# A two-model float32 stack on one core: gate products in split operands, spread rows by one stacked product, attention heads in alternation

## The reference, cut to what matters

```python
q = apply_rope(q, cos, sin) * (Dh ** -0.5)
k = apply_rope(k, cos, sin)
s_own = einsum('bhqd,bhsd->bhqs', q_c, k_own); p = softmax(where(causal, s_own, -inf))
out = einsum('bhqs,bhsd->bhqd', p, v_own)
```

```python
ig  = ml_i + ml_b_i;   lf  = log_sigmoid(ml_f + ml_b_f)      # 4 + 4 columns
flf = log_sigmoid(fx_f + fx_b_f)                             # 8 columns
cT = cumsum(flf);  s = (q @ k.T) * scale + cT[q] - cT[k]     # forgetting attention, causal
dmat = cumsum(lf)[t] - cumsum(lf)[s] + ig[s]                 # mLSTM, causal
```

## Time and profile before

| what | value |
|---|---|
| median of 3 runs | 1218.9 us |
| the profiled execution | 1219.48 us |
| its span, first to last instruction | 1217.7 us |
| TensorE busy | 1180.7 us |
| VectorE busy | 752.7 us |
| ScalarE busy | 617.7 us |
| TensorE's granted clock, mean | 0.993 |

### The profile page before, as it was taken

One profiled execution on the slowest core, in us unless ns is written; L12 is line 12 of the kernel. 1 busy time (PEld: TensorE's weight loads), 2 busy tenths in 40 slices (PEclk: granted clock), 3 DMA queues, 4 the chain that ended last, 5 costly groups with the idle time before them and its releaser, 6 DMA issues.

```text
span 1217.7 us, 24847 instructions
## 1 busy us (share of the span) xinstructions
PE 1180.7 (97%) x10598; PEld 1064.5 (87%) x10598; DVE 752.7 (62%) x1084; ACT 617.7 (51%) x892; POOL 109.5 (9%) x87
## 2 busy tenths in 40 slices
PE   6999999999999999999999999999999999999997
PEld 6797777789999989997999999799988898999996
DVE  7788775374554467785555444758478564655554
ACT  8974543363434355554643434565545474644443
POOL 0032253601100000220010000000000000000000
PEclk9999989999999999999999999999999999999999
DMA  8522111055544545333455446354432352545551
GB/s 297 209 104 72 27 53 52 20 196 217 193 186 180 206 168 183 129 119 124 173 197 186 178 169 255 109 186 173 152 126 105 138 191 104 206 177 206 188 185 42
DMA packets 29950, 188.17 MB, mean 155 GB/s; under 512 B 3489, under 2 KB 5665, under 8 KB 8737
## 3 DMA queue, kind: packets, MB, share of 16 engines
q1 hardware_dynamic: 27072, 177.21, 39.9%
q10 hardware_dynamic: 2784, 9.60, 2.4%
HBM read 185.75 MB, written 1.05 MB: 153 GB/s over the span
## 4 chain that ended last, share of the span: by engine, by line
PE 86%; DVE 8%; ACT 4%; issue 2%; DMA 0%; ACTq 0%; DVEq 0%; SPq 0%
PE ps L2046 24%; PE ps L2048 24%; PE ps L2047 23%; DVE w_lo L1333 1%; PE ps L2364 1%; PE ps L2179 1%; PE ps L2509 1%; PE ps L2369 1%; PE ps L2542 1%; PE ps L2366 1%; ACT mixed L618 1%; ACT w_hi L720 1%; PE ps L2312 1%; PE ps L2263 1%; PE ps L2762 1%
## 5 line engine op out<-in xcount | busy, mean ns | idle before, releaser
L1333 DVE TENSOR_TENSOR w_lo<-w_raw,w_hi 128x2048 fp32r<-128x2048 f32 x157 | 365.7, 2345 | 147.4 <-ACT w_hi L589 146.8
L2046 PE MATMUL ps<-x_hi,w_hi 128*128 128x256 f32 x1344 | 380.3, 283 | 4.1 <-DVE x_lo L1620 2.4
L2047 PE MATMUL ps<-x_lo,w_hi 128*128 128x256 f32 x1344 | 375.3, 279 | 0.0
L2048 PE MATMUL ps<-x_hi,w_lo 128*128 128x256 f32 x1344 | 375.1, 279 | 0.0
L589 ACT CAST w_hi<-w_raw 128x2048 fp32r<-128x2048 f32 x155 | 295.1, 1906 | 155.0 <-PE ps L2048 154.0
L2046 PEld LDWEIGHTS ps<-x_hi,w_hi 128*128 128x128 f32 x1344 | 252.6, 188 | 13.3 <-issue 8.3
L2047 PEld LDWEIGHTS ps<-x_lo,w_hi 128*128 128x128 f32 x1344 | 252.6, 188 | 2.2 <-issue 0.7
L2048 PEld LDWEIGHTS ps<-x_hi,w_lo 128*128 128x128 f32 x1344 | 252.6, 188 | 0.0
L2046 PE MATMUL ps<-w_hi,hid_hi 128*128 128x512 f32 x304 | 119.7, 394 | 0.1
L2048 PE MATMUL ps<-w_hi,hid_lo 128*128 128x512 f32 x304 | 119.4, 393 | 0.0
L2047 PE MATMUL ps<-w_lo,hid_hi 128*128 128x512 f32 x304 | 118.5, 390 | 0.0
(11 more groups left out here) (394 smaller groups left out, 1797.5 us busy)
## 6 DMA issues: line engine op xcount, KB each, us to landing
w_raw<-in_weights SPq DMA_DIRECT2D x163, 1024.0 KB, 4.9
xt<-in_xT SPq DMA_DIRECT2D x2, 512.0 KB, 5.4
w_raw<-in_weights SPq DMA_DIRECT2D x2, 512.0 KB, 6.2
x_tm<-in_x SPq DMA_DIRECT2D x1, 1024.0 KB, 5.2
gain<-in_mix_g ACTq DMA_DIRECT2D x2, 512.0 KB, 4.0
gain<-in_mix_b ACTq DMA_DIRECT2D x2, 512.0 KB, 6.0
gain<-in_ffn_g ACTq DMA_DIRECT2D x2, 512.0 KB, 7.7
gain<-in_ffn_b ACTq DMA_DIRECT2D x2, 512.0 KB, 10.8
```

What stands on the lines that cost most here:

```text
L1333: V.tensor_tensor(w_lo[:, i % WS, :], w_raw[:, i % RAW, :], w_hi[:, i % WS, :].bitcast(F32), ALU.subtract).then_inc(lo_done, 1)
L2046: nc.tensor.matmul(out, hi_l, hi_r, start=start, stop=False)
L2047: nc.tensor.matmul(out, hi_l, lo_r, start=False, stop=False)
L2048: return nc.tensor.matmul(out, lo_l, hi_r, start=False, stop=stop)
```

## The change

The input `gatesel` and its load are gone (so the count of late loads falls from 80 to 64 everywhere). The gate weights are split into `gate_hi` and `gate_lo`, each 36 columns wide (forget gates in 0 to 11, input gates in 32 to 35), which lie in parts of `mix_lo` that are free then; ScalarE and VectorE do it before ffn1. The selector `gsel` is now built on the chip in fp32r, [44, 12, 128]: VectorE adds two pieces of the identity, ScalarE copies it along 128 columns. The two gate products become one split product. The rows are split too: their high part goes to rows 0 to 11 and their low part to rows 32 to 43 of `gst_s` (`gi_s` likewise), and one fp32r product of 44 partitions with the selector, which has a one in row h and in row 32 + h, adds both. In the attentions the heads are in their natural order, slot h for head h, and the products of heads 2m and 2m + 1, which lie on different halves of the partitions, alternate.

```diff
+RS = 44
...
+        gsel = sb("gsel", [RS, 12, P], F32R, a_m)
+        sel = sb("sel", [RS, 12], where=a_m)
...
+        gate_hi, gate_lo = (mix_lo[:, n:n + 2, :].rearrange("p a b -> p (a b)")[:, 0:36 * KT].rearrange("p (k n) -> p k n", k=KT)
+                            for n in (4, 6))
+        gi_s, gst_s = mix_hi[0:RS, 6, :], mix_hi[0:RS, 7, :]
...
-            nc.scalar.dma_start(gsel[:, :], d["const_gates"]).then_inc(late_loaded, 16)
```

ScalarE, between `norm(2)` and `ffn("ffn1")`:

```diff
             load_gain("mix", 1, 2)
+            act.wait_ge(late_loaded, 64)
+            act.wait_ge(slab_done, first["moba_o"] + 4)
+            nc.scalar.copy(gate_hi[:, :, 0:12], gate_w[:, :, 0:12])
+            nc.scalar.copy(gate_hi[:, :, 32:36], gate_w[:, :, 12:16]).then_inc(gate_w_hi, 1)
+            act.wait_ge(sel_set, 1)
+            nc.scalar.copy(gsel[:, :, :], along(sel[:, :], P)).then_inc(gsel_set, 1)
             ffn("ffn1")
```

ScalarE, after the four results of ml_qk are taken:

```diff
+            act.wait_ge(gate_rows, 1)
+            nc.scalar.copy(gst_s[0:12], gst[0:12, :])
+            nc.scalar.copy(gi_s[0:4], gi[0:4, :]).then_inc(row_hi, 1)
             act.wait_ge(mem_loaded, 16)
```

VectorE, before `ffn("ffn1")`:

```diff
+            V.tensor_tensor(sel[:, :], ident[0:RS, 0:12], ident[0:RS, 32:RS], ALU.add).then_inc(sel_set, 1)
+            dve.wait_ge(gate_w_hi, 1)
+            V.tensor_tensor(gate_lo[:, :, 0:12], gate_w[:, :, 0:12], gate_hi[:, :, 0:12].bitcast(F32), ALU.subtract)
+            V.tensor_tensor(gate_lo[:, :, 32:36], gate_w[:, :, 12:16], gate_hi[:, :, 32:36].bitcast(F32), ALU.subtract)\
+             .then_inc(gate_w_lo, 1)
             ffn("ffn1")
```

VectorE, before the convolution:

```diff
+            dve.wait_ge(row_hi, 1)
+            V.tensor_tensor(gst_s[32:RS], gst[0:12, :], gst_s[0:12].bitcast(F32), ALU.subtract)
+            V.tensor_tensor(gi_s[32:36], gi[0:4, :], gi_s[0:4].bitcast(F32), ALU.subtract).then_inc(row_lo, 1)
             dve.wait_ge(p_taken, P_FIRST["ml_qk"] + 4)
```

TensorE, MoBA's scores and outputs (those of the forgetting attention change in the same way):

```diff
-                for s, h in enumerate(HEADS):
-                    q, m = head(h)
+                for m in range(2):
                     for t, c0, c1 in CAUSAL:
-                        last = mm(ps[:, 4 + s, c0:c1], ma_q2[q, m, tok(t)], ma_k2[q, m, 0:c1 - c0], start=True, stop=True)
-                    last.then_inc(scores_ready, 1)
+                        for h in (2 * m, 2 * m + 1):
+                            q = head(h)[0]
+                            last = mm(ps[:, 4 + h, c0:c1], ma_q2[q, m, tok(t)], ma_k2[q, m, 0:c1 - c0], start=True, stop=True)
+                            if t:
+                                last.then_inc(scores_ready, 1)
...
-                for s, h in enumerate(HEADS):
-                    q, m = head(h)
-                    pe.wait_ge(pt_taken, 4 * g + s + 1)
-                    v = lambda t: ma_vv[:, g % 2, t, HD * h:HD * h + HD]
-                    mm(ps[q, bank, T * m:T * m + T], v(0), ma_p[:, s, 0:T], start=True, stop=False)
-                    last = mm(ps[q, bank, T * m + P:T * m + T], v(1), ma_p[:, s, T:T + P], start=False, stop=True)
+                for m in range(2):
+                    pe.wait_ge(pt_taken, 4 * g + 2 * m + 2)
+                    for t in range(TT):
+                        for h in (2 * m, 2 * m + 1):
+                            last = mm(ps[head(h)[0], bank, T * m + P * t:T * m + T], ma_vv[:, g % 2, t, HD * h:HD * h + HD],
+                                      ma_p[:, h, T * t:T + P * t], start=t == 0, stop=t == 1)
```

TensorE, gates and rows:

```diff
-                pe.wait_ge(late_loaded, 80)
+                pe.wait_ge(gate_w_lo, 1)
                 for k in range(KT):
-                    mm(ps[0:12, 3, 0:T], gate_w[:, k, 0:12], x_fm[:, k, :], start=k == 0, stop=k == KT - 1)
-                for k in range(KT):
-                    last = mm(ps[0:4, 3, T:2 * T], gate_w[:, k, 12:16], x_fm[:, k, :], start=k == 0, stop=k == KT - 1)
+                    last = three(ps[0:36, 3, 0:T], gate_hi[:, k, :], gate_lo[:, k, :], x_hi[:, k, :], x_lo[:, k, :],
+                                 k == 0, k == KT - 1)
...
+                    pe.wait_ge(gsel_set, 1)
+                    pe.wait_ge(row_lo, 1)
-                r, src = (4, gi) if n < 4 else (12, gst)
-                mm(ps[:, 3, 0:T], gsel[0:r, P * n:P * n + P], src[0:r, :], start=True, stop=True).then_inc(row_ready, 1)
+                mm(ps[:, 3, 0:T], gsel[:, n, :], gi_s if n < 4 else gst_s, start=True, stop=True).then_inc(row_ready, 1)
```

More of the change, by code:

```diff
@@ L71, in constants @@
     c["onesrow"] = np.ones((P, P))
-    c["gatesel"] = np.concatenate([np.broadcast_to(i == h, (P, P)) for h in range(12)], axis=1)
     return {k: np.ascontiguousarray(v, dtype=np.float32) for k, v in c.items()}
@@ L137 @@
     "rope": ["cos", "sin", "rot"],
-    "gates": ["gatesel"],
 }
@@ L278, in build @@
         conv_in = xk_fm
-        gsel = sb("gsel", [P, 12 * P], where=a_m)
+        gsel = sb("gsel", [RS, 12, P], F32R, a_m)
+        sel = sb("sel", [RS, 12], where=a_m)
         gate_w = sb("gate_w", [P, KT, 16], where=a_m)
         gate_bf = sb("gate_bf", [12, 1], where=a_m)
-        gate_bi = sb("gate_bi", [4, 1], where=a_m)
+        gate_bi = sb("gate_bi", [36, 1], where=a_m)
+        gate_hi, gate_lo = (mix_lo[:, n:n + 2, :].rearrange("p a b -> p (a b)")[:, 0:36 * KT].rearrange("p (k n) -> p k n", k=KT)
+                            for n in (4, 6))
+        gi_s, gst_s = mix_hi[0:RS, 6, :], mix_hi[0:RS, 7, :]
         with ExitStack() as a:
@@ L437, in build @@
         late_loaded = sem("late_loaded")
+        sel_set, gsel_set, gate_w_hi, gate_w_lo, row_hi, row_lo = (
+            sem(n) for n in ("sel_set", "gsel_set", "gate_w_hi", "gate_w_lo", "row_hi", "row_lo"))
         rot_ready, rope_done, scores_ready, masked_ready, exp_ready, p_ready, pt_ready, pt_taken = (
@@ L1813, in _ @@
                 after(first["ffn0"] + i)
-            dve.wait_ge(late_loaded, 80)
+            dve.wait_ge(late_loaded, 64)
             cos, sin = rope_c[:, 0:T], rope_c[:, T:2 * T]
@@ L1863, in _ @@
             link(V.memset(gst[:, :], 0.0))
-            dve.wait_ge(late_loaded, 80)
+            dve.wait_ge(late_loaded, 64)
             dve.wait_ge(gate_mm, 1)
             link(V.tensor_scalar(zf[:, :], ps[0:12, 3, 0:T], gate_bf[:, :], None, ALU.add))
-            link(V.tensor_scalar(gi[0:4, :], ps[0:4, 3, T:2 * T], gate_bi[:, :], None, ALU.add))
+            link(V.tensor_scalar(gi[0:4, :], ps[32:36, 3, 0:T], gate_bi[32:36, :], None, ALU.add))
             V.scalar_tensor_tensor(za[:, :], zf[:, :], -1.0, zf[:, :], ALU.mult, ALU.max).then_inc(gate_abs, 1)
@@ L2520, in rotate @@
                 if g == 0 and n == 0:
-                    pe.wait_ge(late_loaded, 80)
+                    pe.wait_ge(late_loaded, 64)
                 if g > 1 and n == 0:
@@ L2661, in fx_scores @@
                     pe.wait_ge(o_taken, O_FX + 1)
-                for s, h in enumerate(HEADS):
-                    q, m = head(h)
+                for m in range(2):
                     for t, c0, c1 in CAUSAL:
-                        last = mm(ps[:, 4 + s, c0:c1], fx_q[q, 2 * g + m, tok(t)], fx_k[q, 2 * g + m, 0:c1 - c0],
-                                  start=True, stop=True)
-                    last.then_inc(scores_ready, 1)
+                        for h in (2 * m, 2 * m + 1):
+                            q = head(h)[0]
+                            last = mm(ps[:, 4 + h, c0:c1], fx_q[q, 2 * g + m, tok(t)], fx_k[q, 2 * g + m, 0:c1 - c0],
+                                      start=True, stop=True)
+                            if t:
+                                last.then_inc(scores_ready, 1)
             def fx_transposes(g):
@@ L2673, in fx_outputs @@
             def fx_outputs(g):
-                for s, h in enumerate(HEADS):
-                    q, m = head(h)
-                    pe.wait_ge(pt_taken, U_FX + 4 * g + s + 1)
-                    v = lambda t: fx_v[:, t, 256 * g + HD * h:256 * g + HD * h + HD]
-                    mm(ps[q, 4, T * m:T * m + T], v(0), se_p[:, s, 0:T], start=True, stop=False)
-                    last = mm(ps[q, 4, T * m + P:T * m + T], v(1), se_p[:, s, T:T + P], start=False, stop=True)
+                for m in range(2):
+                    pe.wait_ge(pt_taken, U_FX + 4 * g + 2 * m + 2)
+                    for t in range(TT):
+                        for h in (2 * m, 2 * m + 1):
+                            at = slice(256 * g + HD * h, 256 * g + HD * h + HD)
+                            last = mm(ps[head(h)[0], 4, T * m + P * t:T * m + T], fx_v[:, t, at], se_p[:, h, T * t:T + P * t],
+                                      start=t == 0, stop=t == 1)
                 last.then_inc(o_ready, 1)
```

3 lines of the change are left out of this document (1 added, 2 removed).

## The result

| | before | after |
|---|---|---|
| median | 1218.4 us (4 runs, 1215.6 to 1219.3) | 1203.9 us (4 runs, 1200.8 to 1204.2) |
| profiled execution, span | 1219.5, 1217.7 | 1203.8, 1201.9 |

The ratio is 0.9882, interval 0.9857 to 0.9908: 14.5 us less, 11 to 17. The forecast was 1205.3, in a range of 1200.0 to 1209.5.

The account below looks back on a forecast made before the run. TensorE, busy 97% of the span, was taken as the bound. Saving 17.8 us there less 4.2 lost in waits gives 13.6 off 1219.5, 1205.9, and 0.6 less for the median: 1205.3, range 1200.0 to 1209.5.

Parts of the forecast that it names:

- Gates: Gate products on TensorE: 16 f32 products become 24 split ones, 7.44 us falling to 3.35, saving 4.1 (3.9 to 4.3).
- one more change of array shape: At the gates: lower case, one further shape change costs the 0.21 of the way in, saving 3.9 us.
- Rows: Twelve spread rows on TensorE: two records become one split product, 0.41 us saved each, 4.9 in all (3.6 to 8.5).
- Scores 0.76 and outputs 0.70 a group: Attention heads on TensorE, six groups: paired heads run side by side, scores saving 4.6 us in all, outputs 4.2.
- Rival D: Head pairs in scores and outputs take turns instead of running side by side: 1211.9 us, chance 0.10.
- Lost in MoBA: Saved TensorE time given back waiting for VectorE's rotated keys: 0.54 us in MoBA's third group, 0.1 in the second.
- Lost at the eighth row: TensorE's wait for VectorE's bias at the eighth spread row takes 1.6 us of savings, growing from 0.5 to 2.1.
- Lost before the second fx transposes: Forgetting attention's second transposes: nearly all of 2.0 us saved by three rows and a scores block is lost.
- Added work before ffn1, the convolution's delay, the load: Extra ScalarE and VectorE operations, convolution some 1.4 us later, one 768 KB load gone: all costed at nothing.
- Rival C: TensorE's clock falls to half after its waits in forgetting attention, one or two 3.4 us stretches: 1207.0 to 1208.7, chance 0.14.
- B: Nothing is given back, since VectorE's chains move up as well: 1201.1 us, chance 0.16.
- E: TensorE's clock stays down after stalls in the two attentions, making the kernel slower than before: chance 0.03.

## Why the prediction was right, and where its steps were off

**Right as a whole.** From the first scores to the start of the second fx outputs 13.5 us went, and those outputs saved 0.7 more. Less the placement's 0.7 in ffn1, 13.5 us are the change's own, for 13.6 forecast. The rest of the profile's 15.8 is placement (0.7 and 0.8) and 1.0 by which the executions differ ahead of the first scores (in all the traces these start between 473.8 and 479.8), less the 0.2 at the end. Inside the 13.5 TensorE saves 17.4, not 17.8, and 4.1 are lost, not 4.2 (the 0.2 by which these two sums miss the 13.5 lies in differences of 0.02 to 0.06 between stretches). The path was right, but that the number came so near is in part luck: the gates gave 0.3 more and MoBA lost 0.6 less, the rows gave 0.7 less and the second fx transposes lost 0.5 more. The median, 1203.9, is 1.4 below the forecast, about the size of the placement, which no term of it had.

**Gates: 4.1 forecast, 4.4 measured.** The way in and out, kept in the sum, does not exist at 36 columns; "one more change of array shape" did not either.

**Rows: the term that was mis-sized.** 0.41 each forecast, 0.32 measured (1.06 to 0.74, product ahead to second behind), near the lower bound of 0.30. I had put a step of 0.12 in the middle and 0.09 more for the way out; the start behind the row is 0.31 away and the next 0.22. The two rows ahead of scores save more: with the scores behind them they went from 2.80 to 1.53 (from the product ahead of the row to the last product of the scores), 1.27 less, of which 0.76 is the scores' own and 0.51 the row's. Twelve rows are 10 x 0.32 + 2 x 0.51 = 4.2, not 4.9, on TensorE.

**Scores 0.76 and outputs 0.70 a group, as forecast.** Rival D is wrong, for the outputs in their shared bank too. The reason given, alternation, was too narrow: neighbours suffice.

**Lost in MoBA: 0.64 forecast, under 0.1 measured.** It is 5.09 less where 4 x 0.76 + 3 x 0.70 = 5.14 could go. The step "VectorE had only 0.93 idle, the rest being without a gap" took durations as fixed. VectorE and GpSimd in the third group, before:

```profile
529.36 3.14 DVE L1333 TENSOR_TENSOR w_lo<-w_raw,w_hi 128x2048 fp32r<-128x2048 f32 x1 [3.53 <-ACT w_hi L589]
...
529.08 1.27 POOL L1303 TENSOR_TENSOR x_tm<-xn,gain 128x512 f32<-128x512 f32 x1 [16.86 <-PE ps L2558]
530.43 3.21 POOL L1304 TENSOR_TENSOR x_tm<-x_tm,gain 128x512 f32<-128x512 f32 x1
```

and after:

```profile
526.12 2.46 DVE L1346 TENSOR_TENSOR w_lo<-w_raw,w_hi 128x2048 fp32r<-128x2048 f32 x1 [3.48 <-ACT w_hi L594]
...
541.42 2.29 DVE L1346 TENSOR_TENSOR w_lo<-w_raw,w_hi 128x2048 fp32r<-128x2048 f32 x1 [0.22 <-ACT w_hi L594]
...
525.15 1.28 POOL L1316 TENSOR_TENSOR x_tm<-xn,gain 128x512 f32<-128x512 f32 x1 [15.41 <-PE ps L2580]
526.51 3.22 POOL L1317 TENSOR_TENSOR x_tm<-x_tm,gain 128x512 f32<-128x512 f32 x1
```

A low half takes 2.29 alone and 3.14 beside GpSimd. GpSimd's work starts with TensorE's outputs, the low half a little later; after the change more of GpSimd's first operation lies ahead of it, and it takes 2.46, 0.68 less. With the idle 0.93 down to 0.22 VectorE's chain from here to the keys is 1.39 shorter, all but 0.1 of what TensorE saves between two outputs. The first GpSimd operation overlaps the low half by 0.99 before and makes it 0.85 longer, by 0.31 after and makes it 0.17 longer; GpSimd's second operation, which starts inside the low half, takes 3.2 in both, against 1.3 in ffn1, where it starts first. In the whole trace before, the 146 low halves with no GpSimd operation beside them take 2.28 to 2.30; of the eleven with one, ten start behind it and take 3.1 to 3.3, and one starts first and takes 2.29. So whichever of the two starts second is the one that takes longer. That GpSimd is the cause is read from this overlap; no run took it away.

**Lost at the eighth row: 1.6 forecast, 1.58 measured.** VectorE and TensorE after, beside the earlier trace rows:

```profile
884.66 2.29 DVE L1346 TENSOR_TENSOR w_lo<-w_raw,w_hi 128x2048 fp32r<-128x2048 f32 x1 [0.57 <-ACT w_hi L594]
...
888.62 0.42 DVE L1942 TENSOR_TENSOR bias<-bias,base_c 128x256 f32<-128x256 f32 x1
```

```profile
889.10 0.39 PE L2668 MATMUL ps<-mix_hi,gsel 44*128 44x256 f32 x1 [2.07 <-DVE bias L1942]
```

The wait went from 0.49 to 2.07. The second order kernel, which takes the low half and the denominators out of the way and sends the seventh row earlier, took it away.

**Lost before the second fx transposes: 2.0 forecast, 2.5 measured.** From the tenth row to these transposes' end the kernel after takes 0.56 longer (22.11 for 21.55), with 2 x 0.32 + 1.27 = 1.9 less work in it. So a part of the fx outputs' 0.70, which I had counted as kept, went as well. They end before ScalarE can copy them:

```profile
908.96 1.90 ACT L594 CAST w_hi<-w_raw 128x2048 fp32r<-128x2048 f32 x1
909.82 0.38 PE L2668 MATMUL ps<-mix_hi,gsel 44*128 44x256 f32 x1
...
910.76 0.59 ACT L1072 COPY se_o<-ps 128x512 f32<-128x512 f32 x1
...
911.87 0.69 DVE L1811 TENSOR_TENSOR mix_lo<-se_o,mix_hi 128x512 fp32r<-128x512 f32 x1 [2.88 <-ACT mix_hi L1073]
```

The row behind the outputs starts at 909.82, the copy 0.94 later; before the change 0.24 later (924.87 and 925.11). The cast in front of it had been hidden by the slower outputs. The kernel that copies first got 0.8 back.

**Added work before ffn1, the convolution's delay, the load: nothing,** as forecast; TensorE's only wait for a low part at ffn1's start is the 0.2 before the second slab that was there before, and there is none at row 1.

**Rival C.** In the profiled execution it did not come about, and the median's forecast did not need it. For a single execution its chance of 0.14 looks too low: of ten waits of 1.3 us or more at the eighth and the twelfth row, over all traces, four are followed by the fall, at 1.6 us each, or at nothing where a later wait takes it up. Rivals B, D and E did not come about.

**The rules cited.** By the 81 ns of the Trainium skill ("TensorE: Matmul & The Clock Gate", Back-to-back issue gap) for each of its eight 128-column records a block of outputs would take 8 x 0.026 = 0.2 more than the forecast's 1.45, by this estimate 1.66. It took 1.45, so the figure does not hold for these pairs. The Trainium skill's warning that tiling does not speed the engines that empty PSUM ("TensorEngine Tiling (Array Packing)", PSUM Bottleneck) fits two of the three places in its direction: TensorE waits there for VectorE, 1.6 and 2.5 are lost. But what held VectorE and ScalarE up was in good part work that empties no PSUM (a low half at the eighth row, a cast before the copy of the outputs), and in MoBA hardly anything was lost.

## What to carry to other kernels

When TensorE gets faster, the gain stops at the first engine whose list has work in front of what TensorE waits for. Look there for work that nobody needs yet (weight slabs' low halves, a cast) and change the order: such moves and wider rows were worth another 8 us here (456.08 to 448.15 from the first scores to the second fx outputs), over half of what the change itself gave. Give a small product the partitions of its neighbours; beside products on 64 partitions it made no difference here. And compare stretches, not only totals: the kernel before took from 1213.4 us (mean granted clock 0.999) to 1222.9 us (0.989) within one set of 17 runs, and a few bytes of placement are worth 1.5.

## What the hardware showed that I had not expected

- Two heads on different halves run side by side whatever the order of their four products (1.50 against 1.45 us for outputs, 1.61 against 1.51 for scores), and a spread row of 44 partitions right ahead of scores on 64 starts 0.01 us ahead of them.
- Narrow columns (36) cost no way in or out, fewer partitions (44) do: 0.09 in, 0.19 on the row and 0.10 behind it.
- A wait of 1.3 to 2.1 us was followed by half clock (0.50, for 3.4 us) in some executions and not in others, at 1.6 to 1.7 us each where no later wait took it up.
- 48 unused bytes a partition made the 191 us of ffn1 and what surrounds it 0.7 us shorter, and the last 259 us too.
- A VectorE subtraction of 2.29 us took 3.14 us beside GpSimd's elementwise work, by an amount that follows its overlap with GpSimd's first operation.
